# A two-layer encoder step: keys and two query tiles made together in each layer's front

## Chip, cores and metric

The kernel runs on one core of a Trainium2 chip. The metric is device time in microseconds (us) of one execution, the median of several runs: 2521.57 us before the change, from three runs (2517.52 to 2522.04). The engines are TensorE (PE; PEld is its weight load), VectorE (DVE), ScalarE (ACT), GpSimd (POOL) and SyncE (SP, which here only issues DMAs). ACT issues DMAs too, on a queue of its own.

## The reference, cut to what matters

One step of a two-layer trunk over 512 prompt tokens and 64 sample tokens, d_model 2048. Each layer:

```python
mod = jnp.dot(jax.nn.silu(c), w_ada) + b_ada
shift, scale, gate = jnp.split(mod, 3, axis=-1)
h = rmsnorm(x, g) * (1 + scale[:, None]) + shift[:, None]
u = jnp.dot(h, w_in)      # split into xa, za, q/k/v/z of two attentions, qi, ki, wi
...
sc = jnp.einsum('thd,sd->ths', qi, ki) * IDX_DIM ** -0.5
score = jnp.einsum('ths,th->ts', jax.nn.relu(sc), w)
vals, idx = lax.top_k(score, topk)
...
return x + gate * out, new
```

Three groups of heads read h: a gated linear recurrence, a band attention, and a sparse attention whose keys are chosen by the index scores above (16 index heads of 64 in qi, one key of 64 in ki, and weights wi beside it).

## The kernel before, in words

All activations lie transposed, feature by token: `xy`, 16 tiles (k = 0 to 15) of 128 features by 576 tokens. Float32 matmuls are made from three: weights and activations are split into a rounded part and a residual, and hi·hi, hi·lo and lo·hi are added up (L610 to L619). One output tile of the input projection, 128 columns of `w_in`, is 16 k steps of six matmuls in two halves of 288 tokens. Weights come in chunks of four k (256 KB) into a ring of four slots, `raw`: SP loads a chunk when POOL has split the one four places before it (`load`, L380), ACT rounds it into `w_hi` (`upper`, L994) when TensorE has used the slot's last chunk, POOL writes the residual `w_lo` (`split`, L503), TensorE multiplies (`chunks`, L598). Two PSUM tiles, `proj[0]` and `proj[1]`, take turns.

The order of the output tiles in a layer: KI (the index key and weights, 80 columns), QI to QI+7 (the index queries), 16 tiles of the recurrence, 32 of heads, then 16 of the output projection. Every engine runs a program written out in this order by hand, and semaphores tie them.

**The front of layer 0.** x is loaded and transposed by TensorE (L534); DVE copies it into `xy`. POOL squares the 16 tiles and adds them (L487 to L493), TensorE sums over features with ones (`sum_squares`, L548), DVE makes mean and reciprocal (`mean_square`, L1370), ACT the root (L992). Beside it the vector c is multiplied with the first 4096 columns of `w_ada`, in eight blocks j of 512 columns. A block is 4 MB and comes in four slots s of 1 MB (L357); a slot is loaded again once its last product is made. `modulate(j)` multiplies a block into one of two PSUM slots, `read_rows(j)` copies the row to SBUF, `turn_modulation(j)` transposes it. Two blocks give shift and scale for one chunk of four k: `take_modulation(c)` adds bias and scale, then DVE scales four k in place (L1472), ACT rounds them into `act_hi` (`upper_h`, L1005), and POOL (even k) and DVE (odd k) write the residuals `act_lo` (`lower`). TensorE makes KI chunk by chunk between the blocks (L680 to L691). Before x is scaled in place, ACT writes it to DRAM (`x_keep`, L981, four DMAs), and DVE waits for all four (L1458). Also in the front: 20 small vector loads on SP (L346); two DMAs on ACT that build bias windows in DRAM (`rel_windows`, L975, 2 MB) and one that masks them (L978); and DVE's constants of the recurrence's decay for both layers (L1390 to L1418).

**The front of layer 1.** The sum of squares comes from the end of layer 0. DVE scales one k after the other (L1478 to L1488); TensorE makes KI as chunks of the input get ready (L693 to L696), then the query tiles.

**Behind the front.** Query tile q holds its 16 k steps, the rotation of tile q-1 (`swap` on TensorE, then `rotate` on DVE) and the scores of earlier tiles (`score`, `relus`, `add_scores`). The remaining columns of `w_ada` come in narrow blocks of 256 columns, one in each tile (`late`, `late_take`, `load_late`; 24 blocks in layer 0, 8 in layer 1).

Of the kernel before, what the change touches and what calls it, by code (L numbers as in the profile page):

```python
# [49 lines left out]
LATE_AT = (0, 3 * AT)  # L50
A_ROW, A_MOD = HALF, HALF + 132
# [22 lines left out]
def build(nc, inp, out, scratch):  # L74

    with ExitStack() as ctx:
# [97 lines left out]
        r_x = lb[2][:, 0:T]  # L174
# [17 lines left out]
        x_kept = sem("x_kept")  # L192
        x_whole = sem("x_whole")
# [13 lines left out]
        ada_read = sem("ada_read", 2)  # L207
# [70 lines left out]

        def t_no(h, e):


            return 3 + 8 * h + e + (0 if h < 5 else min(e + 1, 4) if h == 5 else 4)
# [24 lines left out]
        CONSTS = 4  # L307
# [3 lines left out]
        def _(sp):  # L311
            for s, n in started:
                sp.sem_inc(s, n)
            for dst, src in (
# [4 lines left out]
                sp.dma_start(dst, src).then_inc(c_in, 16)  # L319

            for i in range(10):
                b, slot, cols = i // 2, i % 5, slice(i % 2 * XC, (i % 2 + 1) * XC)
# [4 lines left out]
            for dst, src in (  # L327
                (ones[:, :], inp["ones"]), (swap_i[:, :], inp["swap_i"]), (swap_d[:, :], inp["swap_d"]),
# [4 lines left out]
            for l in range(DEPTH):  # L333

                for n, (name, row, rows) in enumerate((
                    ("b_ada", V1["b_ada"], ADA), ("g_norm", V1["g_norm"], KT),
                    ("conv_w", V1["conv_w"], 4 * G), ("conv_b", V1["conv_b"], G),
                    ("b_rg", V1["b_rg"], G), ("b_ig", V1["b_ig"], G), ("lru_lambda", V1["lam"], G),
                    ("g_branch", V2["g_branch"], KT), ("state_lru", V2["state_lru"], G),
                    ("state_conv", V2["state_conv"], 3 * G),  # L340
                )):
                    src = inp[name][l]
                    src = {1: lambda a: a.rearrange("(r p) -> r p", p=P),
                           2: lambda a: a.rearrange("a (r p) -> (a r) p", p=P),
                           3: lambda a: a.rearrange("a b (r p) -> (a b r) p", p=P)}[len(src.shape)](src)
                    sp.dma_start(vrow_of[l][row:row + rows, int(n > 6), :], src).then_inc(vec_in, 16)  # L346
# [29 lines left out]
            for l in range(DEPTH):  # L376
# [18 lines left out]
                for q in range(8):  # L395
                    load(w_in, QI + q, COL_QI + q * P, cs=(0, 1))
                    if q > 1:
                        load_late(l, q - 1)
                    load(w_in, QI + q, COL_QI + q * P, cs=(2, 3))
                    if q == 0:  # L400
                        load_late(l, 0)
# [1508 lines left out]
```

## Time and profile before

| what | value |
|---|---|
| median of 3 runs | 2521.57 us |
| profiled execution, own time | 2520.9 us |
| its span, first to last instruction | 2518.8 us |
| mean granted TensorE clock | 0.953 |
| TensorE busy | 2347.0 us, 93% of the span |
| weight load busy | 2172.3 us, 86% |
| DVE, ACT, POOL busy | 1012.9, 809.4, 856.1 us |
| DMA moved | 312.07 MB, mean 124 GB/s |
| chain that ended last | TensorE 88%, DVE 4%, DMA 4% |

How to read it: times in rows are from the span's start. The granted clock is a share of full speed; 0.50 is 1.2 GHz and 1.00 is 2.4 GHz, and means between are mixtures of the two. "idle before <-X" says that the engine sat idle that long before the instruction and that X ended the wait.

### The profile page before, as it was taken

How to read it: one execution, taken by the hardware profiler on the slowest of the kernel's cores; microseconds unless marked ns; L12 is line 12 of the kernel's file. 1: busy time of each engine (PE TensorE's matmuls, PEld its weight loads, DVE VectorE, ACT ScalarE, POOL GpSimd, SP SyncE). 2: the span in 40 equal slices, each digit the busy share in tenths (PEclk: the TensorE clock that was granted, in tenths of full speed). 3: DMA queues.
4: the chain of work that ended last, by engine and by line, in shares of the span. 5: the costliest groups of instructions: out<-in, count | busy, mean ns of one | idle time of the engine just before them, and what ended most of it. 6: DMA issues, size and time to landing. Idle time of an engine off the chain costs nothing.

```text
span 2518.8 us, 47056 instructions
## 1 busy us (share of the span) xinstructions
PE 2347.0 (93%) x18247; PEld 2172.3 (86%) x18247; DVE 1012.9 (40%) x1900; ACT 809.4 (32%) x1543; POOL 856.1 (34%) x651
## 2 busy tenths in 40 slices
PE   4589999999999999979994999999999999997997
PEld 2278889999999998969994887999999999987997
DVE  7434456664211223451117345677411123353113
ACT  0123334433333333332222333444433333333221
POOL 5222223333333332334433322343433333343441
PEclk6689999999999999979996999999999999998999
DMA  8975556663333332214432652333333332322443
GB/s 289 356 221 162 169 160 194 199 197 108 101 92 86 84 81 77 73 60 134 129 110 67 189 162 57 78 84 81 95 89 92 95 83 78 79 66 81 130 130 136
DMA packets 442878, 312.07 MB, mean 124 GB/s; under 512 B 21305, under 2 KB 413377, under 8 KB 441481
## 3 DMA queue, kind: packets, MB, share of 16 engines
q1 hardware_dynamic: 415064, 283.35, 38.4%
q10 hardware_dynamic: 27632, 26.21, 3.3%
q8 instruction: 126, 2.06, 0.3%
q14 instruction: 56, 0.45, 0.1%
HBM read 280.81 MB, written 30.92 MB: 124 GB/s over the span
## 4 chain that ended last, share of the span: by engine, by line
PE 88%; DVE 4%; DMA 4%; issue 2%; DVEq 1%; POOL 1%; ACT 1%; ACTq 0%; SPq 0%; POOLq 0%
PE proj L612 25%; PE proj L614 24%; PE proj L618 24%; PE proj L630 2%; PE misc L676 2%; PE misc L828 2%; PE misc L801 2%; PE proj L661 1%; PE misc L746 1%; DMA rel_windows<-rel_rows 1%; PE misc L810 1%; DMA work<-in_w_ada 1%; DMA x_keep<-xy 1%; PE proj L641 1%; DVE act_lo L1319 1%
## 5 line engine op out<-in xcount | busy, mean ns | idle before, releaser
L612 PE MATMUL proj<-act_hi,w_hi 128*128 128x288 f32 (+1 forms) x4672 | 1341.4, 302 | 63.2 <-issue 34.0
L614 PE MATMUL proj<-act_lo,w_hi 128*128 128x288 f32 (+1 forms) x4672 | 1314.8, 297 | 0.0
L507 POOL TENSOR_TENSOR w_lo<-raw,w_hi 128x512 fp32r<-128x512 f32 (+1 forms) x584 | 765.2, 1313 | 1444.6 <-ACT w_hi L1000 1444.0
L618 PE MATMUL proj<-act_hi,w_lo 128*128 128x288 f32 (+1 forms) x4672 | 1004.9, 297 | 0.0
L612 PEld LDWEIGHTS proj<-act_hi,w_hi 128*128 128x128 f32 (+1 forms) x4672 | 884.9, 189 | 113.1 <-issue 99.9
L614 PEld LDWEIGHTS proj<-act_lo,w_hi 128*128 128x128 f32 (+1 forms) x4672 | 885.5, 190 | 3.0
L618 PEld LDWEIGHTS proj<-act_hi,w_lo 128*128 128x128 f32 (+1 forms) x4672 | 754.5, 189 | 0.0
L1000 ACT ACTIVATE w_hi<-raw 128x512 fp32r<-128x512 f32 (+1 forms) x584 | 364.2, 628 | 1153.7 <-PE proj L618 1126.3
L1322 DVE SCALAR_TENSOR_TENSOR acc<-work,kw_tok,acc 128x256 f32<-128x256 f32 (+3 forms) x128 | 103.5, 809 | 148.4 <-ACT work L1066 142.5
L1322 DVE SCALAR_TENSOR_TENSOR xy<-misc,hg,xy 128x512 f32<-128x512 f32 (+1 forms) x32 | 16.5, 517 | 243.7 <-PE misc L828 243.2
L1322 DVE SCALAR_TENSOR_TENSOR xy<-proj,mod,lb 128x224 f32 (+5 forms) x72 | 25.6, 411 | 210.9 <-PE proj L618 210.9
L500 POOL TENSOR_TENSOR act_lo<-xy,act_hi 128x576 fp32r<-128x576 f32 x32 | 51.5, 1624 | 151.7 <-ACT act_hi L1009 100.4
L1322 DVE SCALAR_TENSOR_TENSOR work<-misc,work 128x128 f32<-128x128 f32 (+4 forms) x40 | 19.6, 490 | 184.1 <-PE misc L801 181.0
L565 PE MATMUL misc<-work,sc 128*2 128x512 f32 x256 | 47.6, 857 | 40.6 <-DMA work<-in_w_ada 40.6
L1319 DVE TENSOR_TENSOR sqb<-sqb,sq 128x576 f32<-128x576 f32 (+2 forms) x66 | 54.1, 820 | 70.7 <-ACT sq L959 40.3
L1165 ACT ACTIVATE work<-work,nmx 128x128 f32<-128x128 f32 (+4 forms) x80 | 45.1, 564 | 111.4 <-DVEq L1681 111.3
L1023 ACT ACTIVATE work<-misc 128x512 f32<-128x512 f32 (+5 forms) x176 | 63.7, 389 | 30.4 <-PE misc L810 15.1
L565 PEld LDWEIGHTS misc<-work,sc 128*2 128x2 f32 x256 | 4.9, 90 | 76.3 <-DMA work<-in_w_ada 48.7
L828 PEld LDWEIGHTS misc<-work 128*128 128x128 f32 (+1 forms) x416 | 57.4, 196 | 14.8 <-issue 11.4
L828 PE MATMUL misc<-work 128*128 128x128 f32 (+2 forms) x416 | 64.4, 284 | 3.4 <-ACT sq L1215 3.4
L630 PE MATMUL proj<-xy,sc 128*2 128x128 f32 x2048 | 61.7, 272 | 0.0
L630 PEld LDWEIGHTS proj<-xy,sc 128*2 128x2 f32 x2048 | 50.4, 85 | 11.8 <-issue 9.9
(192 smaller groups left out, 1755.5 us busy)
## 6 DMA issues: line engine op xcount, KB each, us to landing
raw<-in_w_in SPq DMA_DIRECT2D x448, 256.0 KB, 2.9
xy<-in_w_ada SPq DMA_DIRECT2D x64, 1024.0 KB, 7.7
work<-in_w_ada SPq DMA_DIRECT2D x32, 1024.0 KB, 10.4
raw<-in_w_out SPq DMA_DIRECT2D x128, 256.0 KB, 2.8
x_keep<-xy ACTq DMA_DIRECT2D x32, 288.0 KB, 2.5
lb<-x_keep SPq DMA_DIRECT2D x24, 288.0 KB, 3.2
x_keep<-xy ACTq DMA_DIRECT2D x4, 1152.0 KB, 12.8
out_y_prompt<-work SPq DMA_DIRECT2D x4, 1024.0 KB, 3.9
```

The costliest lines, as they stand in the source:

```text
L500: pool.tensor_tensor(act_lo[:, k, :], xy[:, k, :], act_hi[:, k, :].bitcast(F32), ALU.subtract).then_inc(h_low_g, 1)
L507: pool.tensor_tensor(w_lo[:, c, :, 0:width], raw[:, c, :, 0:width], w_hi[:, c, :, 0:width].bitcast(F32), ALU.subtract)\
L565: m = pe.matmul(s_ps[j % 2][32 * kk:32 * kk + 2, :], sc[:, s * KC + kk, :], ada_w[:, s, kk, :], start=(s == 0), stop=(s == 3), tile_positi ...
L612: pe.matmul(dst, w_hi[:, c, kk, 0:width], act_hi[:, k, cols], start=(k == 0), stop=False)
L614: pe.matmul(dst, w_hi[:, c, kk, 0:width], act_lo[:, k, cols], start=False, stop=False)
L618: m = pe.matmul(proj[b][0:width, half, 0:HALF], w_lo[:, c, kk, 0:width], act_hi[:, k, cols], start=False, stop=(k == KT - 1))
L630: m = pe.matmul(proj[b][32 * kk:32 * kk + 2, half, A_ROW:A_ROW + P], sc[:, u * 8 + k, :], late_w[:, u, k, half * P:(half + 1) * P], start= ...
L828: m = pe.matmul(o_ps[:, c:c + NQ[b]], v, p_t[b % 2][0:v.shape[0], j * P:j * P + NQ[b]], start=(j == 0), stop=(j == len(vs) - 1), skip_grou ...
L1000: act.activation(w_hi[:, c, :, 0:width], raw[:, c, :, 0:width], ACT.Copy)\
L1023: act.activation(dst, src, ACT.Copy)
L1319: return dve.tensor_tensor(o, a, b, op)
L1322: return dve.scalar_tensor_tensor(out=o, in0=a, scalar=s, in1=b, op0=op0, op1=op1)
```

## The change

`FRONT = 3` tiles, KI, QI and QI+1, are made together in each layer's front, chunk by chunk of the input; n = 3c + t numbers their 12 weight chunks. KI goes to `proj[1]`, QI to `proj[0]`, QI+1 to the first half of `misc`. In layer 0 a w_ada slot and one k step (`quarter`) alternate, and w_ada's product has one PSUM slot (`o_ps`) instead of two.

Beside it: the squares of layer 0 move from POOL to ACT, four buffers, and TensorE adds them up with ones; x comes half by half of the features; the vector loads move to ACT's queue, the ones to an early DMA; `x_keep` is written and waited for chunk by chunk; the window DMAs and the decay constants move to later places; the key lies in `ki_raw` instead of `qi_raw`; the late w_ada blocks start two tiles later and end in head 0.

SP, loads:

```diff
+            def load_front(l, n):
+
+                c, t = n // FRONT, n % FRONT
+                w, col = front_width(n), COL_KI if t == 0 else COL_QI + (t - 1) * P
+                hold(sp, lo_ready, l * CHUNKS + n + 1 - RING)
+                sp.dma_start(raw[:, n % RING, :, 0:w], inp["w_in"][l].rearrange("(k p) n -> p k n", p=P)
+                             [:, c * KC:(c + 1) * KC, col:col + w]).then_inc(raw_in[n % RING], 16)
...
             for j in range(HALF_ROWS):
                 col = (j // 2 + j % 2 * (KT // KC)) * AB
-                if j == 4:
-                    sp.wait_ge(xt_read, 20)
-                    for c in range(4):
-                        sp.dma_start(raw[:, c, :, 0:80],
-                                     inp["w_in"][0].rearrange("(k p) n -> p k n", p=P)
-                                     [:, c * KC:(c + 1) * KC, COL_KI:COL_KI + 80]).then_inc(raw_in[c], 16)
                 for s in range(4):
                     if j > 0:
                         hold(sp, ada_used, 4 * j + s - 3)
                     sp.dma_start(ada_w[:, s], w_ada[:, s * KC:(s + 1) * KC, col:col + AB])\
                         .then_inc(ada_in[s], 16)
+                if j == 1:
+                    sp.wait_ge(xt_read, 20)
+                for n in ((), (0, 1, 2, 3), (4, 5, 6, 7), (), (), (8, 9), (), (10, 11))[j]:
+                    load_front(0, n)
```

POOL (`FRONT_CHUNKS` is ((0, 1, 2, 3), (4,), (5, 6, 7), (8, 9, 10), (11,))):

```diff
-            pool.tensor_tensor(sqx, xy[:, 0, :], xy[:, 0, :], ALU.mult)
-            for k in range(1, KT):
-                pool.tensor_tensor(sq[:, :], xy[:, k, :], xy[:, k, :], ALU.mult)
-                pool.drain()
-                pool.tensor_tensor(sqx, sqx, sq[:, :], ALU.add)
...
+                for c in range(5):
+                    if c > 0:
+                        lower(l, 0, (c - 1) * KC, c * KC)
+                    for n in FRONT_CHUNKS[c]:
+                        split_front(l, n)
```

TensorE:

```diff
+            def add_up(k):
+
+                pe.wait_ge(x_squared, k + 1)
+                for half in range(2):
+                    m = pe.matmul(proj[0][:, half, 0:HALF], ones[:, :],
+                                  squares[k % 4][:, half * HALF:(half + 1) * HALF],
+                                  start=(k == 0), stop=(k == KT - 1))
+                m.then_inc(square_used if k < KT - 1 else ss_made, 1)
...
+            for e in range(12):
+                turn_x(e)
+            pe.wait_ge(ones_in, 16)
+            pe.wait_ge(c_ready, 1)
+            for e in range(12, 20):
+                turn_x(e)
+                add_up(e - 12)
+            for k in range(8, KT):
+                add_up(k)
...
+            def modulate(j, s):
+
+                if s == 0 and j > 0:
+                    hold(pe, ada_read, j)
+                hold(pe, ada_in[s], (j + 1) * 16)
...
             hold(pe, vec_ready, 1)
+            for j in range(2):
+                for s in range(4):
+                    modulate(j, s)
             turn_modulation(0)
             turn_modulation(1)
...
+                for c in range(3):
+                    parts = [(n, kk) for n in range(FRONT * c, FRONT * c + FRONT) for kk in range(KC)]
+                    for i in range(8):
+                        if l == 0:
+                            modulate(2 * c + 2 + i // 4, i % 4)
+                        quarter(*parts[i])
+                    quarter(*parts[8])
+                    if l == 0:
+                        turn_modulation(2 * c + 2)
+                        turn_modulation(2 * c + 3)
+                    for n, kk in parts[9:]:
+                        quarter(n, kk)
+                for n in (9, 10):
+                    for kk in range(KC):
+                        quarter(n, kk)
+                swap(KI, 1, swap_i[0:64, 0:64], ki_raw, 64)
...
+                for kk in range(KC):
+                    quarter(11, kk)
+                swap(QI, 0, swap_i[:, :], qi_raw, P)
```

`quarter(n, kk)` is one k step of `chunks`: six matmuls, which wait for the residual of that one k.

ACT (the 20 vector loads stand unchanged at the start of its program, ahead of the Tanh; `keep_first(c)` is the DMA of x_keep's quarter c):

```diff
-            decay(0)
-            decay(1)
+            act.activation(rinv[:, 0:1], eps[:, :], ACT.Sqrt)
+            for k in range(KT):
+                if k % 8 == 0:
+                    act.wait_ge(xt_read, 10 * (k // 8 + 1))
+                hold(act, square_used, k - 3 if k > 3 else 0)
+                act.activation(squares[k % 4], xy[:, k, :], ACT.Square).then_inc(x_squared, 1)
+            keep_first(0)
...
+                for c in range(5):
+                    if c > 0:
+                        upper_h((c - 1) * KC, c * KC)
+                    if l == 0 and 0 < c < 4:
+                        keep_first(c)
+                    for n in FRONT_CHUNKS[c]:
+                        upper_front(n)
+                    if l == 0 and c == 0:
+                        decay(0)
+                        decay(1)
+                        act.wait_ge(rel_out, 16)
+                        act.dma_start(scratch["windows"],
+                                      bass.AP(scratch["rows"].tensor, 0, [[640, 8], [1, P], [1, 512]]))\
+                            .then_inc(rel_out, 16)
```

DVE (`vectors(l)` are the decay constants of one layer):

```diff
+            mean_square(proj[0], r_x, D_MODEL, 1)
             hold(dve, vec_made, 2)
...
-                    for k in range(KT):
-                        tt(xy[:, k, :], xy[:, k, :], r_x, ALU.mult)
-                    dve.drain()
                     for c in range(4):
+                        hold(dve, x_first[c], 16)
+                        for k in range(c * KC, (c + 1) * KC):
+                            tt(xy[:, k, :], xy[:, k, :], r_x, ALU.mult)
+                        take_modulation(c)
                         for k in range(c * KC, (c + 1) * KC):
                             for a, z, w in PARTS:
                                 dve.tensor_scalar(xy[:, k, a:z], xy[:, k, a:z], mod[:, KT + k, w:w + 1],
                                                   mod[:, k, w:w + 1], ALU.mult, ALU.add)
                             dve.drain().then_inc(norm_x, 1)
+                        lower(c * KC + 1, 0)
+                        lower(c * KC + 3, 0)
+                        if c in (1, 2):
+                            vectors(c - 1)
```

## Rows read from the trace of the kernel before

**Rows 1.** The page, busy share of TensorE in 40 equal slices of the span, in tenths.

```profile
PE   4589999999999999979994999999999999997997
```

**Rows 2.** Busy time by stages of layer 0's front; columns named in the first line.

```profile
core 0: us, PE busy (x) PEld busy (x) DVE busy (x) ACT busy (x) POOL busy (x), PEclk, DMA share, GB/s
...
35.90:61.40 25.50, 11.32 (x48) 0.67 (x48) 22.87 (x41) 0.00 (x0) 22.94 (x19) 0.50 0.97 363
...
111.00:122.00 11.00, 5.19 (x32) 0.45 (x32) 0.69 (x1) 0.55 (x1) 1.15 (x1) 0.74 1.03 381
```

**Rows 3.** TensorE's timeline, layer 0's front: start, duration, instruction, idle before.

```profile
17.39 1.97 PE L544 MATMUL misc<-ident,raw 128*128 128x128 f32 x8 [1.75 <-DMA raw<-in_x_prompt]
...
30.63 1.88 PE L565 MATMUL misc<-work,sc 128*2 128x512 f32 x8 [1.50 <-DMA work<-in_w_ada]
...
72.97 1.24 PE L551 MATMUL proj<-sqb,ones 128*128 128x288 f32 x4
84.76 1.89 PE L565 MATMUL misc<-work,sc 128*2 128x512 f32 x8 [10.55 <-DMA work<-in_w_ada]
...
122.59 3.58 PE L574 MATMUL misc<-sel,sqb 128*128 128x2 f32 x16
...
145.70 1.04 PE L565 MATMUL misc<-work,sc 128*2 128x512 f32 x8 [1.67 <-DMA work<-in_w_ada]
...
165.10 0.29 PE L612 MATMUL proj<-act_hi,w_hi 128*128 128x288 f32 x1
...
171.51 1.18 PE L661 MATMUL proj<-qi_raw,swap_i 64*64 64x288 f32 x4
172.62 0.41 PE L704 MATMUL misc<-ident,ci 128*64 128x128 f32 x2
```

**Rows 4.** TensorE's timeline, layer 1's front: KI's first chunk and the first query matmul.

```profile
1347.13 0.50 PE L612 MATMUL proj<-act_hi,w_hi 128*80 128x288 f32 x1 [23.23 <-DVE act_lo L1319]
...
1348.63 0.44 PE L612 MATMUL proj<-act_hi,w_hi 128*80 128x288 f32 x1
...
1350.07 0.44 PE L612 MATMUL proj<-act_hi,w_hi 128*80 128x288 f32 x1
...
1351.97 0.29 PE L612 MATMUL proj<-act_hi,w_hi 128*80 128x288 f32 x1
...
1377.12 0.29 PE L612 MATMUL proj<-act_hi,w_hi 128*128 128x288 f32 x1
```

**Rows 5.** DVE's timeline, layer 0's front: decay constants, reciprocal, scalings, residuals.

```profile
30.00 0.17 DVE L1392 TENSOR_SCALAR hg<-vec 128x16 f32<-128x16 f32 x1
...
61.40 1.39 DVE L1418 TENSOR_SCALAR sp<-sp 128x8 f32<-128x8 f32 x1
...
75.16 3.75 DVE L1375 RECIPROCAL lb<-lb 128x576 f32<-128x576 f32 x1
84.46 10.79 DVE L1319 TENSOR_TENSOR xy<-xy,lb 128x576 f32<-128x576 f32 x16 [5.55 <-DMA x_keep<-xy]
...
146.81 0.69 DVE L1383 COPY sqb<-misc 128x512 f32<-128x512 f32 x1 [11.35 <-PE misc L565]
...
152.14 4.39 DVE L1472 TENSOR_SCALAR xy<-xy,mod 128x512 f32<-128x512 f32 x8
156.65 3.59 DVE L1319 TENSOR_TENSOR act_lo<-xy,act_hi 128x576 fp32r<-128x576 f32 x2
```

**Rows 6.** DVE's timeline, layer 1's front: pairs of scalings of k = 1, 3 and 15.

```profile
1335.55 0.65 DVE L1484 TENSOR_SCALAR xy<-xy,mod 128x512 f32<-128x512 f32 x2
...
1339.15 1.62 DVE L1484 TENSOR_SCALAR xy<-xy,mod 128x512 f32<-128x512 f32 x2
...
1370.64 1.64 DVE L1484 TENSOR_SCALAR xy<-xy,mod 128x512 f32<-128x512 f32 x2
```

**Rows 7.** The chain of waits (windows); below, DMA issues at 62.0 to 62.5 us.

```profile
35.86 25.51 DMA rel_windows<-rel_rows
...
x_keep<-xy ACTq DMA_DIRECT2D x1, 1152.0 KB, 9.2
```

**Rows 8.** Waits of TensorE at 1530 to 1580 us: total, times, longest.

```profile
PE misc L746 <- issue: 4.6, 1, 4.6
```

More of the change, by code:

```diff
@@ L192, in build @@
         x_kept = sem("x_kept")
+        x_first = [sem(f"x_first{c}") for c in range(4)]
+        x_squared = sem("x_squared")
+        square_used = sem("square_used", 4)
+        ones_in = sem("ones_in")
         x_whole = sem("x_whole")
@@ L306, in build @@
         TOK = 32 * 16
-        CONSTS = 4
+        CONSTS = 3
+        squares = [sqb[:, n, :] for n in range(3)] + [sq[:, :]]
+        front = (proj[1], proj[0], misc[:, 0:2, :])
         @block.sync
@@ L319, in _ @@
                 sp.dma_start(dst, src).then_inc(c_in, 16)
+            sp.dma_start(ones[:, :], inp["ones"]).then_inc(ones_in, 16)
             for i in range(10):
-                b, slot, cols = i // 2, i % 5, slice(i % 2 * XC, (i % 2 + 1) * XC)
+                b, slot, cols = i % 5, i % 5, slice(i // 5 * XC, (i // 5 + 1) * XC)
                 if i >= 5:
@@ L387, in _ @@
                 if l > 0:
-                    load(w_in, KI, COL_KI, 80)
+                    for n in range(4 * FRONT):
+                        load_front(l, n)
                     hold(sp, roped, l * 17)
@@ L619, in chunks, with quarter @@
                                               act_hi[:, k, cols], start=False, stop=(k == KT - 1))
+                        m.then_inc(chunks_used, 1)
+                def quarter(n, kk):
+                    c, t = n // FRONT, n % FRONT
+                    k, at, w = c * KC + kk, n % RING, front_width(n)
+                    if t == 0:
+                        pe.wait_ge(h_low_g, l * KT + k // 2 + 1)
+                        if k > 0:
+                            pe.wait_ge(h_low_v, l * KT + (k + 1) // 2)
+                    if n < 2:
+                        pe.wait_ge(bank_free[1 - n], l * USES[1 - n] + 1)
+                    if n == 2 and l > 0:
+                        hold(pe, r_ready, l * 5)
+                    if kk == 0:
+                        pe.wait_ge(lo_ready, l * CHUNKS + n + 1 + RING)
+                    for half in range(2):
+                        cols = slice(half * HALF, (half + 1) * HALF)
+                        dst = front[t][0:w, half, 0:HALF]
+                        pe.matmul(dst, w_hi[:, at, kk, 0:w], act_hi[:, k, cols], start=(k == 0), stop=False)
+                        pe.matmul(dst, w_hi[:, at, kk, 0:w], act_lo[:, k, cols], start=False, stop=False)
+                    for half in range(2):
+                        cols = slice(half * HALF, (half + 1) * HALF)
+                        m = pe.matmul(front[t][0:w, half, 0:HALF], w_lo[:, at, kk, 0:w], act_hi[:, k, cols],
+                                      start=False, stop=(k == KT - 1))
+                    if kk == KC - 1:
                         m.then_inc(chunks_used, 1)
@@ L705, in _ @@
                 m.then_inc(t_made, 1)
-                late(0, 1)
-                chunks(QI, 1, 0, (2, 3))
+                for kk in range(KC):
+                    quarter(11, kk)
+                swap(QI, 0, swap_i[:, :], qi_raw, P)
                 hold(pe, roped, l * 17 + 1)
@@ L1036, in _ @@
+                hold(act, chunks_used, l * CHUNKS + 10)
+                hold(act, tok_out, l * TOK)
+                take(KI, 1, [(halves(ki_raw[0:80, :]), wide(proj[1])[0:80])], False)
+                upper(QI + 2, (0,))
+                t_take(0, [(ki_t[64 * n:64 * n + 64, SEQ:NEW_K], t_ps[0:64, 0:2 * P]) for n in range(2)])
+                upper(QI + 2, (1,))
+                hold(act, chunks_used, l * CHUNKS + 11)
                 hold(act, zs_ready, l * 16)
[L1037 removed]
```

393 lines of the change are left out of this document (194 added, 199 removed).

## Prediction

> **What bounds the kernel now.** I read the page first: TensorE is busy nine tenths or more in nearly every slice, and the low digits stand at the start (4, 5, 8) and in the middle (4) [rows 1]. Those are the fronts of the two layers, where a layer's modulated input is not ready; elsewhere TensorE is the bound. So a matmul moved into a front costs nothing and takes its time off the dense part, as long as the front gets no longer. Then the busy time by stages of layer 0's front: at 35.9 to 61.4 us the DMA engines are 0.97 busy while TensorE works 11 of 25 us at a granted clock of 0.50, that is 1.2 GHz; at 111 to 122 us DMA is the bound again (1.03) [rows 2]. Then TensorE's timeline: w_ada's slots (1 MB each) come from 30.63 on; after 72.97 TensorE waits 10.55 us for the next block, the last slot is multiplied at 145.70, the keys end at 165.10, and from there the work is dense [rows 3]. Layer 1: TensorE waits 23.23 us until 1347.13, and query tile 0 starts at 1377.12 [rows 4].
>
> **The measure.** The change makes keys (KI), query 0 and query 1 before the dense part starts. Two chunks of query 0 take 165.10 to 171.51, so a tile takes 12.85, and the swap of KI with the transposes of ci 1.5 (171.51 to 172.96) [rows 3]. Today the same work would be done, without the late w_ada steps that only move, at 165.1 + 25.7 + 1.5 = **192.3** in layer 0 and 1377.1 + 27.2 = **1404.3** in layer 1 [rows 3, 4]. The new fronts are measured against these.
>
> **Layer 0, start.** The 20 vector loads move from SP's queue to ACT's; there they stand ahead of the Tanh for which DVE waits before it copies x. I take 2 us of delay (between 0, if ACT issues at once, and 6). Sums of squares leave POOL: ACT squares, and TensorE adds 16 tiles with ones, 8 of them between the last x transposes. Such a pair of matmuls took 1.24 us [rows 3]; four transposes take 1.0 at half clock, since eight took 1.97 [rows 3], so about 0.5 at full clock. From about 20 us: two rounds at half clock (2.9 each), six at full (1.5), a wait for the last copy and square (2), then eight more at 1.0: the sum stands at about **45**, and now at 74.2. Bounds: 41 at full clock throughout, 61 at half. Behind it on DVE come mean and reciprocal, 4.7 us (74.2 to 78.9) [rows 3, 5], and only then the vector copies (about 1 us), for which the first w_ada product waits: it starts at **51**, not 30.63. Meanwhile block 0 lies in its four slots and no further block can be loaded, so about 15 us of DMA time are lost. This is the price of the new start.
>
> **Layer 0, first chunk.** Block 0 takes 4 x 1.89 at half clock [rows 3] to 58.6. Block 1 is loaded as its slots come free and is used up at about 67.5. Then turns of two blocks 3.5 [rows 3], bias and scale 0.9, eight scalings 4.4 [rows 5]: the first quarter of the input is scaled at N0 = **76**.
>
> **Layer 0, the loop.** Call Nc the end of the scalings of chunk c. DVE does now, in this order: two residuals (1.5 to 3.6 [rows 5]), for c = 1 and 2 the decay constants of one layer, the wait for x_keep's next quarter, four multiplications by r (0.68 each, 10.79 for 16 [rows 5]), and the read of the next block's row (0.7 [rows 5]). Only after this read may TensorE start the second block of the pair, because one PSUM slot is left. The decay constants took 31 to 33 us for both layers while POOL squared beside them (30.00 to 62.8 [rows 5]); that is 16 each, and 26 operations of 0.17 and their drains would be 6.5. POOL only works a part of that time now, so I take 8. The copy of the next quarter of x is issued behind this chunk's ACT casts (1 us) and took 9.2 us to land under load [rows 7]. So the read is done at Nc + 13. Then four slots and five k steps: TensorE has waited, so it starts at half clock (1.89 a slot, and 1.44 a step: 1348.63 to 1350.07), and the clock is up 4.8 us later, as at 1351.97 [rows 4]; from there 1.04 and 0.80: 10.5. Turns 3.5, bias 0.9, scalings 4.4: 19.3. A pair of blocks takes **32**. By DMA it would take 27: a slot is 2.75 us at the 381 GB/s of 111 to 122 us [rows 2], eight of them 22, weights and a quarter of x 5. So DMA no longer bounds the loop.
>
> **The first round is longer.** rel_windows is now copied after ACT's first four weight casts and the decay exponentials, at about 72. That copy took 25.5 us beside w_ada [rows 7]. The second quarter of x_keep is issued at 77 on the same ACT queue behind it. I take that it lands when the windows have, at about **100** (bounds: 77 + 9 = 86, and 106 if it takes its 9 us after the windows). So N1 = 100 + 2.8 + 0.7 + 19.3 = 123, N2 = 155, N3 = 187. The end behind N3 is two residuals, the last key step, and two query chunks with the swap between: 1.7 + 0.9 + 3.2 + 1.5 + 3.2, and about 2 for the clock, which has fallen in the wait (as behind the wait before 1347.13 [rows 4]): 12.5. The front ends at 199.5, against 192.3: **7 us lost**. Bounds: if every wait but DMA were gone, from 53 on w_ada's remaining 28 slots (77), the weights (6), x_keep (10) and the half of 25.5 us that the windows took from w_ada (13) end at 159, and the front some 20 later, as now 145.70 to 165.10, at 179: 13 won; with half clock throughout, 36 lost (third rival).
>
> **Layer 1.** Nothing of DMA is in the way; DVE scales one k step in 2.6 us (twelve from 1339.15 to 1370.64 [rows 6]) and TensorE gets 3 x 0.80 = 2.4 us of work for it. The keys of a chunk wait for their k, but query 0 and 1 of a chunk fill the time to the next. From 1347 on TensorE is dense: 5 us at half clock, then full, and by TensorE alone the three tiles end at 1386.5. DVE may be later: a pair of scalings takes 0.65 alone and 1.62 where a POOL residual lies beside it [rows 6], and seven POOL splits of query weights now fall into this stretch: 7 x 0.97 = 6.8. Now the last residual is done at 1373.9 (1377.1 less 3.2). So 1373.9 + 6.8 + 0.8 + 7.9 = 1389.4, against 1404.3: **15 us won** (bounds: 18 if the splits cost nothing; none at half clock, fourth rival).
>
> **Small terms.** The late w_ada products move by two tiles (in layer 0 the last ones into head 0) and cost what they did. In layer 1 one of them now lies before the gates of group 0, where TensorE waited 4.6 us [rows 8]; it covers some, I take 1.4 won (0 to 2.4). SP's earlier issue of block 0, the moved clears of sqb and the scale-up of layer 1 cost nothing: DVE is idle most of head 0, and without that cover they would cost under 2. The evacuations of the three tiles and the score steps for queries 0 and 1 lie beside 6.4 us of query 2's matmuls; I see no wait there (up to 2 if ACT is late).
>
> **Sum.** 7 - 15 - 1.4 = -9.4. The profiled execution took 2520.9 us (span 2518.8), 0.7 below the median 2521.57: **2511.5 us**, 0.4% less. A measurement of this kernel can tell about 0.2%, 5 us, from no change.
>
> **The rivals.**
> First, my forecast: layer 0 gives back part of what layer 1 wins. Chance 0.55, 2503 to 2520.
> Second, **the x copy is not held behind the windows**: it lands at 86, N1 is 109, everything in layer 0 is 14 earlier: 2497; at the DMA bound, 2491. For it: of the four x copies issued from 62.1 us on the first landed after 9.2 us [rows 7], so copies overlap with other traffic. Against it: the last of them let DVE go only at 84.46 [rows 5], so on one queue they came in turn. Chance 0.22.
> Third, slower: **TensorE stays at 1.2 GHz in layer 0's front**, because its matmuls now come in pieces between waits. The sums end at 61 instead of 45 (16), and each pair's second block takes 14.8 instead of 10.5 (3 x 4.3 = 13): 29 more, 2540; it makes the change a loss from 14 more on, which the sums alone would reach (2527). For it: the clock was 0.50 through 25 us in which TensorE worked 11 [rows 2]. Against it: the sums and the interleaved steps are denser than that. Chance 0.15.
> The Trainium skill (TensorE: Matmul & The Clock Gate, HAM oscillation) says that a loop with DMA waits between its tiles is throttled anew in every turn. By that rule the third rival's price would be due in full; the trace agrees where waits are frequent [rows 2] and shows the clock rising within 4.8 us of dense steps [rows 4].
> Fourth, **layer 1 does not do what it should**: at half clock 48 steps x 1.44 are 69 us from 1336 on, ending at 1405, no better than now: 2520.9 + 7 - 1.4 = 2526.5. Against it: 1351.97, and the steps there are dense. Chance 0.08.
>
> **The numbers.** Faster by over 0.2%: 0.41 of the forecast's 0.55 and all of the second's 0.22: 0.63. Within: 0.13, 0.02 of the third and 0.04 of the fourth: 0.19. Slower: 0.01, 0.13 and 0.04: 0.18. The range takes in most of the second case below and the sums' half of the third above: 2490 to 2528. The forecast's own range is 2503 to 2520.
>
> **What would show it.** In the changed profile: the sum of squares ends near 45 and the first w_ada product starts near 51; DVE's multiplication of the second quarter waits for x_keep until about 100; the last w_ada slot is multiplied near 178; the first matmul of query tile 2 comes at about 201 in layer 0; in layer 1 it comes 15 us earlier, counted from the first sum of squares there, than 27 us behind today's start of query 0. A last w_ada slot before 160 would make me wrong towards faster, a first product behind 60 or a granted clock of 0.5 through the front towards slower; a loss in layer 1 would overturn the sign.

## The result, and the profile after

The changed kernel took 2499.42 us (median of 4 runs, 2495.63 to 2499.93) beside 2521.78 for the kernel before: a ratio of 0.9912, with a 95% interval of 0.9895 to 0.9929. It is 22.4 us faster, more than twice the 9.4 that I forecast. The profiled execution took 2499.93 us, with a span of 2498.1; the spans differ by 20.7.

The page of the changed kernel: the low digits stand at the start and in the middle as in [rows 1] (6, 6, 7 and 5 where it had 4, 5, 8 and 4):

```profile
PE   6679999999999999979995999999999999987997
```

TensorE in layer 0's front (timeline: start, duration, instruction, idle before):

```profile
20.47 1.14 PE L559 MATMUL proj<-sqb,ones 128*128 128x288 f32 x4
...
38.73 1.13 PE L559 MATMUL proj<-sq,ones 128*128 128x288 f32 x4
...
45.41 6.42 PE L587 MATMUL misc<-work,sc 128*2 128x512 f32 x32 [4.80 <-DVEq L1529]
...
93.93 1.89 PE L587 MATMUL misc<-work,sc 128*2 128x512 f32 x8 [14.32 <-DVE sqb L1491]
...
126.02 1.89 PE L587 MATMUL misc<-work,sc 128*2 128x512 f32 x8 [7.22 <-DVE sqb L1491]
...
156.55 1.89 PE L587 MATMUL misc<-work,sc 128*2 128x512 f32 x8 [6.34 <-DVE sqb L1491]
...
188.40 1.13 PE L708 MATMUL proj<-qi_raw,swap_i 128*128 128x288 f32 x4
```

L559 adds up squares, L587 is w_ada's product, L708 the swap; the swap of query 0 is the end of the front in this text. Where [rows 3] had waits for w_ada, TensorE now waits for DVE's reading of a block's row (L1491), in each of the three rounds. What DVE does meanwhile (L1428 with `ki_t` is the multiplication by r, L1576 the scalings of a chunk):

```profile
68.05 4.40 DVE L1576 TENSOR_SCALAR xy<-xy,mod 128x512 f32<-128x512 f32 x8
...
90.51 2.77 DVE L1428 TENSOR_TENSOR xy<-xy,ki_t 128x576 f32<-128x576 f32 x4 [15.43 <-DMA x_keep<-xy]
...
107.45 4.41 DVE L1576 TENSOR_SCALAR xy<-xy,mod 128x512 f32<-128x512 f32 x8
...
122.61 2.75 DVE L1428 TENSOR_TENSOR xy<-xy,ki_t 128x576 f32<-128x576 f32 x4
...
138.85 4.42 DVE L1576 TENSOR_SCALAR xy<-xy,mod 128x512 f32<-128x512 f32 x8
```

So N0, N1, N2 (the ends of the scalings) are 72.45, 111.86 and 143.27; N3 is 173.87. DVE waits for x_keep once, 15.43 us; in the next two rounds the decay constants (7.1 and 6.2 us) stand in that place. ACT's DMA queue shows why the first is long:

```profile
36.03 0.38 ACTq L1053 DMA_DIRECT2D x_keep<-xy  x1
...
67.84 0.78 ACTq L1120 DMA_DIRECT2D rel_windows<-rel_rows  x1
...
72.52 4.68 ACTq L1053 DMA_DIRECT2D x_keep<-xy  x1
...
111.93 0.37 ACTq L1053 DMA_DIRECT2D x_keep<-xy  x1
```

The quarter behind the windows took 4.68 us to issue alone and landed after 18.0 us; the next one, with nothing ahead of it, 0.37 and 6.8.

Layer 1, TensorE, from the sum of squares to the swap of query 0:

```profile
1315.03 2.29 PE L577 MATMUL proj<-sqb,ones 128*128 128x288 f32 x4 [3.62 <-DVEq L1931]
...
1329.58 0.53 PE L660 MATMUL proj<-act_hi,w_hi 128*80 128x288 f32 x1 [12.26 <-POOL act_lo L502]
...
1353.57 0.33 PE L660 MATMUL proj<-act_hi,w_hi 128*80 128x288 f32 x1 [1.65 <-DVE act_lo L1428]
...
1366.84 0.50 PE L660 MATMUL proj<-act_hi,w_hi 128*80 128x288 f32 x1 [3.57 <-DVE act_lo L1428]
...
1387.31 1.13 PE L708 MATMUL proj<-qi_raw,swap_i 128*128 128x288 f32 x4
```

The front takes 72.28 us here (1315.03 to 1387.31). In the kernel before the sum of squares starts at 1321.62:

```profile
1321.62 2.29 PE L551 MATMUL proj<-sqb,ones 128*128 128x288 f32 x4 [3.62 <-DVEq L1812]
```

So the measure of the prediction has 1404.3 - 1321.62 = 82.7 for the same work.

**Where the 20.7 us come from.** Layer 0's front ends at 188.4 against 192.3: 3.9. The rest of layer 0 gives 2.7 (the sum of squares of layer 1 moved from 1321.62 to 1315.03, 6.6 in all). Layer 1's front gives 10.4, the wait before the gates of group 0 (the matmuls behind a wait in [rows 8]) 1.4 (4.61 us ahead of 1571.53 to 3.18 ahead of 1551.83), and the remainder of layer 1 2.3.

That the 2.7 and the 2.3 come from the change is not shown: in two executions of one other kernel (layer 1 by tiles, below) the stretch between the fronts took 1126.5 and 1129.4 us, and in two of the changed kernel the part behind layer 1's front 1110.8 and 1108.5.

### The profile page after: what moved, and what is told of

It reads as the page before. It is cut to its first block, busy times and chain, and to the rows that moved or that the text cites. A ratio compares the mean times of both kernels' runs of the same rounds, so it can differ in the third digit from the quotient of the medians.

```text
span 2498.1 us, 47131 instructions
## 1 busy us (share of the span) xinstructions
PE 2345.8 (94%) x18307; PEld 2172.4 (87%) x18307; DVE 1000.3 (40%) x1899; ACT 819.2 (33%) x1560; POOL 817.6 (33%) x620
## 4 chain that ended last, share of the span: by engine, by line
PE 89%; DVE 5%; issue 2%; DMA 2%; DVEq 1%; POOL 1%; ACT 1%; ACTq 0%; POOLq 0%
PE proj L633 24%; PE proj L635 23%; PE proj L639 23%; PE proj L677 2%; PE misc L723 2%; PE misc L885 2%; PE misc L858 2%; PE proj L708 1%; PE misc L805 1%; PE misc L587 1%; PE misc L867 1%; DVE act_lo L1428 1%; DMA x_keep<-xy 1%; PE proj L688 1%; DVE xy L1431 1%
## 5 line engine op out<-in xcount | busy, mean ns | idle before, releaser
L633 PE MATMUL proj<-act_hi,w_hi 128*128 128x288 f32 x4480 | 1279.3, 300 | 25.5 <-issue 18.8
L635 PE MATMUL proj<-act_lo,w_hi 128*128 128x288 f32 x4480 | 1254.9, 296 | 0.0
L509 POOL TENSOR_TENSOR w_lo<-raw,w_hi 128x512 fp32r<-128x512 f32 x560 | 735.0, 1314 | 1395.5 <-ACT w_hi L1075 1394.8
L639 PE MATMUL proj<-act_hi,w_lo 128*128 128x288 f32 x4480 | 959.9, 296 | 0.0
L633 PEld LDWEIGHTS proj<-act_hi,w_hi 128*128 128x128 f32 x4480 | 847.0, 189 | 67.7 <-issue 55.3
L635 PEld LDWEIGHTS proj<-act_lo,w_hi 128*128 128x128 f32 x4480 | 847.7, 189 | 3.0
L639 PEld LDWEIGHTS proj<-act_hi,w_lo 128*128 128x128 f32 x4480 | 721.6, 189 | 0.0
L1428 DVE TENSOR_TENSOR sqb<-sqb,sq 128x576 f32<-128x576 f32 (+2 forms) x66 | 53.7, 814 | 72.6 <-ACT sq L1031 39.6
L660 PEld LDWEIGHTS proj<-act_hi,w_hi 128*128 128x128 f32 (+1 forms) x128 | 25.7, 201 | 61.3 <-issue 31.1
L587 PE MATMUL misc<-work,sc 128*2 128x512 f32 x256 | 42.2, 749 | 39.0 <-DVE sqb L1491 28.7
L660 PE MATMUL proj<-act_hi,w_hi 128*128 128x288 f32 (+1 forms) x128 | 44.3, 357 | 32.7 <-POOL act_lo L502 16.4
L517 POOL TENSOR_TENSOR w_lo<-raw,w_hi 128x512 fp32r<-128x512 f32 (+1 forms) x24 | 31.1, 1310 | 129.9 <-ACT w_hi L1085 129.9
```

The costliest lines, as they stand in the source:

```text
L509: pool.tensor_tensor(w_lo[:, c, :, 0:width], raw[:, c, :, 0:width], w_hi[:, c, :, 0:width].bitcast(F32), ALU.subtract)\
L587: m = pe.matmul(o_ps[32 * kk:32 * kk + 2, :], sc[:, s * KC + kk, :], ada_w[:, s, kk, :], start=(s == 0), stop=(s == 3), tile_position=(0, ...
L633: pe.matmul(dst, w_hi[:, c, kk, 0:width], act_hi[:, k, cols], start=(k == 0), stop=False)
L635: pe.matmul(dst, w_hi[:, c, kk, 0:width], act_lo[:, k, cols], start=False, stop=False)
L639: m = pe.matmul(proj[b][0:width, half, 0:HALF], w_lo[:, c, kk, 0:width], act_hi[:, k, cols], start=False, stop=(k == KT - 1))
L660: pe.matmul(dst, w_hi[:, at, kk, 0:w], act_hi[:, k, cols], start=(k == 0), stop=False)
```

## The experiments

Measured ratios are to the kernel before, run on the same chip, with their interval in square brackets and the median in us in round ones; the changed kernel has 0.9912 [0.9895, 0.9929] (2499.42). The intervals of most single edits overlap with this one, so what an edit is worth is read from positions in its trace. These scatter too: in five traces with the changed kernel's layer 0 its front ends at 187.7 to 191.4 us, which is 142.9 to 144.4 us after the first w_ada product.

**Windows late.** The theory: the wait of 15.43 us is the queue behind the windows, as I had forecast. The rival: the copy only shared the DMA engines.

```diff
                         decay(0)
                         decay(1)
+                    if l == 0 and c == 3:
                         act.wait_ge(rel_out, 16)
                         act.dma_start(scratch["windows"],
...
```

> Edit: the 2 MB copy of the bias windows is issued on ACT's queue behind the last x_keep quarter (chunk 3) instead of at 67.8 us; its mask follows it before query tile 3. Theory A (the second x_keep quarter is held behind the windows on ACT's queue): it is issued at about 72.5 and lands after 5 to 7 us, as the third and fourth did (6.8), near 79 instead of 90.5; DVE's wait of 15.4 us before its multiplication falls to about 4, the chunk-1 scalings end near 101 instead of 111.9, the layer-0 front near 178 to 180 instead of 188.4; time 2488 to 2492 (2 us given back where the windows now compete with w_ada's last blocks). Theory B (the copy took 18 us only because all transfers shared the DMA engines): it still lands at 88 or later, time 2497 to 2501.

Measured: ratio 0.9885 [0.9867, 0.9903] (2489.66). On DVE, then on TensorE:

```profile
80.46 3.83 DVE L1429 TENSOR_TENSOR xy<-xy,ki_t 128x576 f32<-128x576 f32 x4 [5.16 <-DMA x_keep<-xy]
...
85.42 1.89 PE L587 MATMUL misc<-work,sc 128*2 128x512 f32 x8 [5.26 <-DMA work<-in_w_ada]
...
178.71 1.13 PE L708 MATMUL proj<-qi_raw,swap_i 128*128 128x288 f32 x4
```

The same copy, issued at 72.73, lands after 7.7 us instead of 18.0, and the front is 9.7 us shorter (133.0 us after the first w_ada product). So the windows held x_keep, and theory B, that the traffic beside it would make it late without them too, falls. The edit takes the windows off ACT's queue and off the DMA engines at once, though, so how much of the 10.3 us was order on the queue and how much sharing of the engines with the windows stays open; 4.3 of them lie in the issuing on ACT's queue (4.68 against 0.39). The Trainium skill (DMA: Bandwidth & Descriptors, Queues, rings and completion order) says that each SDMA engine takes the descriptors of one ring in order, with one row of rings per issuing engine; this pair of runs agrees (18.0 and 7.7 us) but does not prove it. Chunk 1 ended at 103.2, not 101: x came at 80.46 instead of 79, its four multiplications took 3.83 us where the changed kernel took 2.77, and TensorE started 0.5 us behind DVE's read (84.89), because of w_ada.

**x_keep early.**

```diff
-            keep_first(0)
+            for c in range(4):
+                keep_first(c)
...
-                    if l == 0 and 0 < c < 4:
-                        keep_first(c)
```

> Edit: all four x_keep quarters are issued together behind the squares (36 us), where the changed kernel leaves the DMA engines nearly idle; nothing else moves. Theory A (the wait for x_keep in the first round is on the path): the four land by about 52, DVE never waits for them, the second block of the first pair starts 11 to 14 us earlier, chunk-1 scalings end at 98 to 102, and the front ends 9 to 13 us earlier: 2486 to 2491. Theory B (the loop is bound by the bytes of w_ada and the windows): the row of block 2 is read earlier, but TensorE then waits for slots of w_ada; scalings of chunk 1 at 106 or later, gain 2 to 5 us, 2494 to 2498. If the later pairs (31.4 and 30.6) depended on their x quarters, they would get shorter too; I expect no change there, since DVE did not wait.

Measured: ratio 0.9909 [0.9889, 0.9929] (2495.04). DVE does not wait for x any more (it multiplies at 74.94), but TensorE does, for w_ada, beside the windows' copy. The chain of waits, and the instruction behind it:

```profile
76.38 13.61 DMA work<-in_w_ada
```

```profile
90.12 1.89 PE L587 MATMUL misc<-work,sc 128*2 128x512 f32 x8 [10.72 <-DMA work<-in_w_ada]
```

Chunk 1 ends at 108.1 and the front at 184.66, 3.7 us earlier (139.8 after the first w_ada product, so 3.1 below the range above). The ratio does not differ from the changed kernel's. By the positions theory B holds: two waits stood side by side, and removing x_keep's bared that of w_ada, 3.8 us shorter (93.93 to 90.12). The pairs stayed at 31.6 and 30.5.

**Decay constants early.**

```diff
                 root(r_x, 0)
+                if l == 0:
+                    decay(0)
+                    decay(1)
...
+                if c == 0:
+                    vectors(0)
                 read_rows(2 * c)
+                if c == 0:
+                    vectors(1)
                 read_rows(2 * c + 1)
...
-                        if c in (1, 2):
-                            vectors(c - 1)
```

> Edit: DVE makes the decay constants of both layers while TensorE multiplies blocks 0 and 1 (ACT's exponentials right behind the root), not in the rounds of chunks 1 and 2. Theory A (the path of a pair goes through DVE: residuals, decay constants, x, read of the row): the read in rounds 1 and 2 is freed of 7.1 and 6.2 us, and then waits for the x quarter (issue at the scalings' end plus 1, 6.8 to land), so each of the two pairs gets 3 us shorter (31.4 to 28.4, 30.6 to 27.6); the start loses 0 to 2; time 2493 to 2497. Theory B (w_ada's slots bound these pairs): the pairs stay at 30.5 or more, time 2499 to 2502.

Measured: ratio 0.9902 [0.9883, 0.992] (2494.66). The ends of the scalings are 72.66, 111.19, 141.16 and 168.61: the pairs fall from 31.4 to 30.0 and from 30.6 to 27.5, and DVE waits for x instead:

```profile
119.81 3.01 DVE L1429 TENSOR_TENSOR xy<-xy,ki_t 128x576 f32<-128x576 f32 x4 [4.91 <-DMA x_keep<-xy]
```

The front ends at 183.17, 5.2 us earlier (137.9 after the first product). Theory A holds, with less in the second round (the copy took 8.5 us there).

**Both.** The two edits above together.

> Both edits: x_keep's four quarters behind the squares, the decay constants beside blocks 0 and 1. Theory A (DVE's chain was the bound, and DMA is next): no wait of DVE for x, no decay constants between; first round as in e2 (98 to 102), the two other pairs at 25 to 27 us (eight slots of 2.75 and weights 2 to 3), scalings of chunk 3 at 150 to 155 instead of 173.9, time 2476 to 2483. The sum of the two edits alone would be 12 to 17 us; more than the sum would show that each covered the other. Theory B (bytes): from 47 us on 28 slots, 3 MB of weights and 4 MB of windows at 350 GB/s end at 152, scalings of chunk 3 at 160 or later, time 2484 or more.

Measured: ratio 0.9846 [0.9823, 0.9869] (2482.39); scalings of chunks 1 to 3 end at 109.75, 134.08 and 157.45, the pairs take 24.3 and 23.4, the front ends at 171.33:

```profile
171.33 1.13 PE L708 MATMUL proj<-qi_raw,swap_i 128*128 128x288 f32 x4
```

That is 17.1 us earlier where the two alone sum to 8.9: each covered the other. Theory A holds for the pairs; the first round stays long (109.75, not 98 to 102). From the end of chunk 0's scalings it takes 36.6 us here and 28.9 in the run with all edits below, where the windows are late too.

**Layer 1 by tiles.** Layer 0 as changed; in layer 1 KI, query 0 and query 1 one after the other.

```diff
+        def front_place(l, n):
+
+            return (n // FRONT, n % FRONT) if l == 0 else (n % 4, n // 4)
```

with the loads, roundings and splits in that order.

> Edit: layer 1 alone goes back to tile after tile (KI, then query 0, then query 1); layer 0 stays changed. The changed kernel's layer-1 front took 72.3 us from the first matmul of the sum of squares to the swap of query 0, where the kernel before would have needed 82.7 for the same work. Theory A (the interleaving alone wins these 10.4): the front takes 81 to 84 again, DVE's scalings go back from 52 to about 44 us, because no POOL splits of query weights lie beside them, and the time is 2507 to 2512. Theory B (what layer 1 won came from the clock or from layer 0's new state): 72 to 75 stay, 2498 to 2503.

Measured: ratio 0.9926 [0.9909, 0.9942] (2503.98), 4.6 us above the changed kernel and less than the trace said: from the first key step to the swap of query 0 it took 69.5 us, the changed kernel 57.7. So both kernels ran again, in five rounds side by side.

> The changed kernel, unaltered, in five rounds beside the run of layer 1 by tiles: the ratio of both is wanted on one chip. Expected 2498 to 2501; the layer-0 front at 187 to 190 and the layer-1 front at 72 us from its sum of squares, as before.

> Layer 1 by tiles once more: the trace of its first run showed a front 11.8 us longer (first key step to the swap of query 0: 69.5 us, not 57.7), its median only 4.6 us more. Theory A: the 11.8 us are the path, and the median differs by 10 to 12 us from the changed kernel in the same call. Theory B: something behind the front takes part of it back (or the clock does), and the medians differ by 3 to 7 us.

Measured: the changed kernel 0.991 [0.9894, 0.9926] (2498.44), layer 1 by tiles 0.9957 [0.9943, 0.997] (2511.18): 12.7 us apart, theory A, a little beyond its 12. In the traces the front, from the sum of squares to the swap of query 0, took 83.2 and 82.0 us by tiles and 72.3 in both traces of the changed kernel. So by the traces the interleaving of layer 1 is worth 10 to 11 us of the 22; by the medians it is 4.6 where the two were not run side by side and 12.7 where they were.

**Narrow splits.** In layer 1 POOL's splits of chunks 4 to 11 take one column; the weight residual of the other columns is left out there.

```diff
-                w = front_width(n)
+                w = front_width(n) if l == 0 or n < 4 else 1
                 pool.wait_ge(hi_ready, l * CHUNKS + n + 1)
```

> Edit: in layer 1 POOL's splits of front chunks 4 to 11 take one column of 128 (or 80), so the weight residual of the other columns of query 0, query 1 and the key is left out (stale) there. Theory A (POOL's splits and DVE's scalings slow one another, more than the 0.97 us each that I charged): DVE's 16 scalings fall from 52.0 to 44 to 46 us, the front from 72.3 to 64.5 to 67, the time by 5 to 8 us to 2491 to 2495. Theory B (TensorE's own work or the act_lo residuals bound it): DVE gets faster, the front stays at 70 to 72.5, time 2497 to 2501.

Measured: ratio 0.9892 [0.987, 0.9914] (2494.05); the swap of query 0 comes 65.1 us after the sum of squares (1315.31 to 1380.36), not 72.3. DVE in 1322 to 1376 us by line and shape (busy us, mean ns), first the changed kernel, then narrow splits, then layer 1 by tiles (first run):

```profile
L1431 DVE SCALAR_TENSOR_TENSOR xy<-xy,mod,ki_t 128x512 f32<-128x512 f32 x16 | 14.1, 878 | 1.9 <-ACT ki_t L1067 0.9
L1590 DVE TENSOR_SCALAR xy<-xy,mod 128x512 f32<-128x512 f32 x16 | 13.0, 813 | 1.3
L1590 DVE TENSOR_SCALAR xy<-xy,mod 128x64 f32<-128x64 f32 x16 | 8.5, 528 | 0.0
L1431 DVE SCALAR_TENSOR_TENSOR xy<-xy,mod,ki_t 128x64 f32<-128x64 f32 x16 | 8.3, 516 | 0.0
L1428 DVE TENSOR_TENSOR act_lo<-xy,act_hi 128x576 fp32r<-128x576 f32 x8 | 8.1, 1026 | 0.8
```

```profile
L1431 DVE SCALAR_TENSOR_TENSOR xy<-xy,mod,ki_t 128x512 f32<-128x512 f32 x16 | 12.4, 777 | 1.9 <-ACT ki_t L1067 0.9
L1590 DVE TENSOR_SCALAR xy<-xy,mod 128x512 f32<-128x512 f32 x16 | 10.6, 663 | 1.4
L1590 DVE TENSOR_SCALAR xy<-xy,mod 128x64 f32<-128x64 f32 x16 | 8.6, 536 | 0.0
L1428 DVE TENSOR_TENSOR act_lo<-xy,act_hi 128x576 fp32r<-128x576 f32 x8 | 8.1, 1027 | 0.8
L1431 DVE SCALAR_TENSOR_TENSOR xy<-xy,mod,ki_t 128x64 f32<-128x64 f32 x16 | 6.2, 387 | 0.0
```

```profile
L1599 DVE TENSOR_SCALAR xy<-xy,mod 128x512 f32<-128x512 f32 x16 | 15.0, 940 | 1.4
L1440 DVE SCALAR_TENSOR_TENSOR xy<-xy,mod,ki_t 128x512 f32<-128x512 f32 x16 | 12.4, 777 | 1.9 <-ACT ki_t L1076 0.9
L1440 DVE SCALAR_TENSOR_TENSOR xy<-xy,mod,ki_t 128x64 f32<-128x64 f32 x16 | 6.2, 387 | 0.0
L1437 DVE TENSOR_TENSOR act_lo<-xy,act_hi 128x576 fp32r<-128x576 f32 x8 | 6.0, 758 | 0.8
L1599 DVE TENSOR_SCALAR xy<-xy,mod 128x64 f32<-128x64 f32 x16 | 4.5, 283 | 0.0
```

The same 72 operations take 52.0, 45.9 and 44.1 us (each the sum of its five rows). So the splits beside them cost DVE 6 to 8 us. What they cost the front is less sure than 7.2: in nine traces with the changed kernel's layer 1 it took 69.8 to 72.4 us, the shorter times where the key step behind the last wait for DVE started at 2.4 GHz (a first matmul of 0.33 or 0.34 us, in four of the nine) and the longer where it started at 1.2 GHz (0.50). With narrow splits it started at 2.4 GHz (0.33), so the splits cost 4.7 to 7.3. Theory A holds. The Trainium skill (SBUF — State Buffer, Who interferes with whom) says that VectorE and GpSimd share a pair of ports, that `tensor_scalar` can hold it for a whole instruction in a two-port mode, and that an operation with two inputs in SBUF contends with what GpSimd reads; the rows of narrow splits agree (777 ns against 878 beside full splits for the second kind, 663 against 813 for the first). By tiles the 512-column `tensor_scalar` takes 940, and only the sum is lower there.

**Vectors copied first.** DVE copies the vectors before mean and reciprocal.

```diff
-            mean_square(proj[0], r_x, D_MODEL, 1)
             hold(dve, vec_made, 2)
...
             dve.drain().then_inc(vec_ready, 1)
+            mean_square(proj[0], r_x, D_MODEL, 1)
```

> Edit: DVE copies the vectors out of PSUM before it makes mean and reciprocal (4.5 us), so that TensorE's first w_ada product waits for neither. Theory A (the late first product is paid in full, since block 1 can be loaded only as slots come free): first product at 41.5 to 42.5 instead of 45.4, everything up to the first scalings 2 to 3.5 us earlier, the layer-0 front ends near 185.5 instead of 188.4; the time 2495 to 2498, not to be told from no change by time alone. Theory B (the root, ready later, or the x copy takes it back): scalings of chunk 0 end at 72 again.

Measured: ratio 0.9889 [0.9864, 0.9914] (2491.97). The first product starts at 41.15 instead of 45.41, the scalings of chunk 0 end at 66.7 instead of 72.45, and the front at 183.33, 5.1 us earlier. Theory A holds, with more than expected: of block 1 three slots were multiplied in one go, in 4.46 us, since they already lay there. Counted from the first product the front takes 142.2 us, about as in the changed kernel (143.0): the gain is in the start. How much of the gain in the median is this edit's, the intervals do not settle.

**All edits of layer 0.** The four edits above, windows, x_keep, decay constants and vector copies, together.

> All edits of layer 0 together: x_keep's quarters behind the squares, decay constants beside blocks 0 and 1, windows copy behind chunk 3, vector copies before mean and reciprocal. Theory A (with DVE's chain and the windows out of the loop w_ada's slots alone are left, 23.4 to 24.3 us a pair as in the run with two of the edits): scalings of chunk 0 end at 70, of chunk 1 at 94 to 97, of chunk 3 at 141 to 145 instead of 157.5, the front at 155 to 159 instead of 171.3; time 2467 to 2473. Theory B (the windows' 2 MB cost as much beside the query weights as beside w_ada): the front ends at 163 or later or query 2 waits for weights, 2476 or more.

Measured: ratio 0.9809 [0.9783, 0.9835] (2471.92); scalings end at 70.9, 99.8, 123.5 and 146.8, the front at 160.62:

```profile
160.62 1.13 PE L708 MATMUL proj<-qi_raw,swap_i 128*128 128x288 f32 x4
```

The pairs (23.6, 23.4) and the time are in theory A's ranges, chunk 1 ends 3 to 6 us later than it said, and the front so 1.6 beyond its range. Busy time by stages (columns as in [rows 2]):

```profile
56.00:67.00 11.00, 7.91 (x52) 3.02 (x48) 6.20 (x30) 2.09 (x4) 4.16 (x4) 0.66 1.08 357
67.00:78.00 11.00, 10.17 (x56) 4.22 (x48) 9.33 (x15) 2.73 (x4) 2.82 (x2) 0.69 1.10 356
78.00:90.00 12.00, 8.91 (x45) 3.82 (x43) 0.09 (x1) 0.63 (x1) 1.26 (x1) 0.72 1.05 387
90.00:100.00 10.00, 9.54 (x77) 6.86 (x76) 5.38 (x16) 2.15 (x4) 1.64 (x2) 1.00 0.96 341
100.00:112.00 12.00, 9.77 (x78) 4.43 (x70) 7.50 (x7) 2.09 (x4) 5.54 (x4) 1.00 1.03 360
```

The DMA engines are busy throughout, and in the first round TensorE waits for w_ada, 3.1 us at the longest. In the two pairs it hardly does: from 99 to 147 us it waits 0.2 us for w_ada, 4.5 for DVE and 1.9 for POOL. So that w_ada's slots set the pace of the pairs, as theory A has it, is not shown. One wait was left in the start, 10.77 us of TensorE for DVE's read of block 0, behind the decay constants. The last edit, on top of these, takes it away:

```diff
-                if c == 0:
-                    vectors(0)
                 read_rows(2 * c)
                 if c == 0:
-                    vectors(1)
+                    vectors(0)
...
                         lower(c * KC + 3, 0)
+                        if c == 3:
+                            vectors(1)
```

> As the run with all edits of layer 0, but layer 0's decay constants are made between the reads of block 0 and block 1, and layer 1's behind the last residual of chunk 3, so that DVE reads block 0 at once (TensorE waited 10.8 us for that read). Theory A (this read held up the start): first scalings end at 66 to 68 instead of 70.9, the front at 156.5 to 158.5 instead of 160.6, time 2467 to 2470. Theory B (DMA is saturated from 36 us on and sets the loop): chunk 1's scalings end at 99 to 100 again and the front at 160 to 161, 2470 to 2473.

Measured: ratio 0.9814 [0.9798, 0.9829] (2473.91), no faster. TensorE now waits there for w_ada:

```profile
55.81 1.89 PE L587 MATMUL misc<-work,sc 128*2 128x512 f32 x8 [8.84 <-DMA work<-in_w_ada]
```

Its first product started 2.5 us later than in the run before it (43.36 to 40.88); counted from there the front takes 120.4 us here and 119.7 there. In the start theory B holds: the wait for DVE's read had covered one for w_ada. The front, at 163.79, lies behind both theories' ranges, by the later start.

## Why the prediction was wrong

The sign was right, the size was not, and the case that I took for the likeliest, layer 0 giving back part of what layer 1 wins, did not come: both fronts won. By the prediction's own steps:

**Layer 0's front, "7 us lost": the step that failed.** It was 3.9 won, 10.9 away. The forecast of -9.4 misses the spans' -20.7 by 11.3; the other misses, 4.6 less in layer 1's front and 5.0 more in stretches that I had put at nothing, nearly cancel. In its pieces, of which the landing of x_keep is the largest:
- *The sum of squares "at about 45", "two rounds at half clock", "a wait for the last copy and square"*: a pair of sums took 0.98 from the first on (20.47, next transpose at 21.45), there was no half clock and no wait, and the sum ended at 39.7, below my lower bound of 41. The first w_ada product came at 45.41, not 51. From there to N0 took 27.0 instead of 25, so N0 is 72.45, not 76.
- *x_keep's second quarter "at about 100"*: that the windows hold this copy was right (windows late shows it), the size not. I had 28 us from the windows' issue (72) to the landing, though [rows 7] have 25.5 for the windows; it was 22.7 (67.84 to 90.5). From the landing to N1 it took 21.4 instead of 23. N0 to N1 took 39.4 instead of 47.
- *"A pair of blocks takes 32"*: 31.4 and 30.6, on the path I had named (decay constants early: -1.4 and -3.1).
- *The end behind N3*: 14.5 instead of 12.5.
- Together: -3.6 - 7.6 - 2.0 + 2.0 = -11.1, from 199.5 to 188.4. The last w_ada slot was multiplied at 164.11, where I had 178.

**Layer 1, "15 us won"**: 10.4. "7 x 0.97 = 6.8" for the splits was 7.8 on DVE (52.0 against the 44.2 that the same five groups sum to in the kernel before), and the last residual came 59.8 us after the sum of squares, where I had 59.1. What failed is "0.8 + 7.9" behind it: 12.45 (1374.86 to 1387.31). TensorE takes its steps in order; it waited 3.57 us for a key's residual, went on at 1.2 GHz (0.45 us a matmul up to 1372, then 0.29), and at the last residual still had two steps of query 1 from the chunk before and all four of the last key chunk in hand, where I had counted one. About 2.3 us of it hang on where the clock fell: four runs with the same layer 1 took 69.8 to 70.1 for this front.

**The gates' wait, "1.4 won"**: 1.4. The small terms at nothing: the part behind layer 0's front gave 2.7, which I had not foreseen. Of it 1.6 is the clock: the gates' eight matmuls and the wait before them are the same, but from their start to the next matmul it took 1.82 us (352.87 to 354.69) and before 3.41 (362.24 to 365.65), at 1.2 GHz for the most part. The change need not be the cause: in the run with narrow splits, whose layer 0 is the changed kernel's, they ran at 1.2 GHz again. First the kernel before, then the changed one, then narrow splits:

```profile
362.24 2.27 PE L746 MATMUL misc<-work,w_rg 128*128 128x290 f32 x4 [3.18 <-issue]
```

```profile
352.87 1.22 PE L805 MATMUL misc<-work,w_rg 128*128 128x290 f32 x4 [3.18 <-issue]
```

```profile
352.17 2.27 PE L805 MATMUL misc<-work,w_rg 128*128 128x290 f32 x4 [3.18 <-issue]
354.23 2.14 PE L805 MATMUL misc<-work,w_ig 128*128 128x290 f32 x4
```

In layer 1 these matmuls account for 1.1 of the remaining 2.3 (from their start to the next matmul 3.59 and 2.47). The cause of the other 1.1 and 1.2 us stays open; executions of one kernel differ by as much (end of the section on the result).

**The rivals.** The second (x_keep not held behind the windows) came near in time, 2497, and for the wrong reason: it was held. The third (1.2 GHz through layer 0's front) was half there: from 56 to 100 us the granted clock was 0.56 to 0.66, but TensorE stood idle in 19 of these 44 us, mostly for DVE's read and w_ada; in the sums (20 to 36 us), and from 100 to 112 us, where steps and slots alternate nearly without waits, it was 1.00. The fourth (no gain in layer 1) fell with layer 1 by tiles.

## What to carry to other kernels

Where several waits end close to one another, take each away alone and together. In the first round x_keep (90.5) covered a wait for w_ada (90.1 once x_keep came early); in the two behind it the decay constants covered x_keep's copies. Alone the two edits were worth 3.7 and 5.2 us, together 17.1. A bulk copy that nobody needs soon goes behind the small copies that somebody waits for, on its queue and in time: this alone was worth 9.7 us of the front. Work moved into another engine's gaps is priced with what it does to the engine beside it: DVE's 72 operations took 52.0 us beside POOL's added splits and 44.1 without.

## What was not expected

The start of TensorE ran at full clock from its first sums, where [rows 2] had 0.50 at 35.9 to 61.4. Issuing a DMA behind a large copy took ACT's queue 4.68 us, not 0.37. And the clock that follows one and the same short wait is not fixed by the program up to there: the gates' eight matmuls up to the next one took 1.82 us in the changed kernel and 3.58 with narrow splits (352.17 to 355.75); medians of four and of five runs of one kernel were 7 us apart (2503.98 and 2511.18, layer 1 by tiles, on two chips), so for edits of this size the positions in the trace, held against their own scatter, told more than a single comparison of times.
